# A two-layer hybrid transformer: tile rows of their own for keys, values and queries, with head sums and rotations inside later slabs

## The reference, cut to what matters

```python
hx = rmsnorm(x, g_pre1[i]) * (1.0 + sc1) + sh1
ux = hx @ w_in[i]
qx = apply_axial_rope(rmsnorm(split_heads(ux[..., :Q_END], N_Q_HEADS), q_norm[i]), rope)
kx, vx = kv_heads(ux[..., Q_END:V_END], k_norm[i], rope)
k_all = jnp.concatenate([kc, kx], axis=1)
v_all = jnp.concatenate([vc, vx], axis=1)
yx = mixer_out(qx, k_all, v_all, ux[..., V_END:P_END], ux[..., P_END:C_END], ux[..., C_END:], lp)
```

## Time and profile before

| | us |
|---|---|
| median of 3 runs | 2336.59 |
| lowest, highest | 2327.56, 2337.27 |
| the profiled execution, its own time | 2337.91 |
| its span, first to last instruction | 2336.1 |
| PE busy in the span | 2143.4 |
| DVE, POOL, ACT busy in the span | 1322.1, 740.4, 737.5 |

### The profile page before, as it was taken

One profiled execution on the slowest core, in us unless ns is written; L12 is line 12 of the kernel. 1 busy time (PEld: TensorE's weight loads), 2 busy tenths in 40 slices (PEclk: granted clock), 3 DMA queues, 4 the chain that ended last, 5 costly groups with the idle time before them and its releaser, 6 DMA issues.

```text
span 2336.1 us, 27666 instructions
## 1 busy us (share of the span) xinstructions
PE 2143.4 (92%) x11298; PEld 1824.1 (78%) x11298; DVE 1322.1 (57%) x1707; ACT 737.5 (32%) x1055; POOL 740.4 (32%) x336
## 2 busy tenths in 40 slices
PE   7889999899999699999999968898879997999997
PEld 6777788678888588888888856677658876888885
DVE  6459899843586566846516544798964314101114
ACT  2447511133222322221112224562124334222222
POOL 3220035132332332222222233103334444444442
PEclk9999999899999699999999978999889997999998
DMA  7110012021344233533223221101222232333322
GB/s 283 37 45 1 19 46 73 22 69 64 122 154 148 78 117 122 172 112 136 99 82 106 93 99 38 44 1 63 73 62 86 100 114 69 98 99 99 98 85 70
DMA packets 62910, 204.44 MB, mean 88 GB/s; under 512 B 7104, under 2 KB 8256, under 8 KB 62528
## 3 DMA queue, kind: packets, MB, share of 16 engines
q1 hardware_dynamic: 56592, 187.72, 24.1%
q10 hardware_dynamic: 6192, 14.95, 1.7%
HBM read 197.40 MB, written 5.24 MB: 87 GB/s over the span
## 4 chain that ended last, share of the span: by engine, by line
PE 70%; DVE 23%; ACT 3%; issue 2%; POOL 1%; DMA 0%; ACTq 0%; DVEq 0%
PE ps L444 61%; DVE conv_acc L1300 11%; PE ps L462 3%; DVE unit_stats L1261 2%; DVE pt0l L1281 1%; DVE pt1l L1281 1%; DVE probs L1275 1%; DVE norm_tmp L1121 1%; PE ps L493 1%; PE ps L615 1%; PE ps L513 1%; PE ps L474 1%; DVE x L1130 1%; PE ps L484 1%; PE ps L636 1%
## 5 line engine op out<-in xcount | busy, mean ns | idle before, releaser
L375 POOL TENSOR_TENSOR w_l<-w_raw,w_h 128x1024 fp32r<-128x1024 f32 (+2 forms) x296 | 675.0, 2283 | 1448.9 <-ACT w_h L749 1448.6
L444 PE MATMUL ps<-h_h,w_h 128*128 128x512 f32 (+1 forms) x1968 | 604.0, 362 | 21.9 <-ACT t L941 17.0
L444 PE MATMUL ps<-h_h,w_l 128*128 128x512 f32 (+1 forms) x1968 | 597.9, 358 | 0.0
L444 PE MATMUL ps<-h_l,w_h 128*128 128x512 f32 (+1 forms) x1968 | 594.3, 357 | 0.0
L444 PEld LDWEIGHTS ps<-h_h,w_h 128*128 128x128 f32 x1968 | 373.9, 190 | 86.1 <-ACT t L941 18.4
L444 PEld LDWEIGHTS ps<-h_l,w_h 128*128 128x128 f32 x1968 | 374.3, 190 | 56.7 <-issue 1.2
L444 PEld LDWEIGHTS ps<-h_h,w_l 128*128 128x128 f32 x1968 | 373.1, 190 | 55.0
L749 ACT ACTIVATE w_h<-w_raw 128x1024 fp32r<-128x1024 f32 (+2 forms) x296 | 281.1, 950 | 207.0 <-PE ps L444 182.6
L1300 DVE SCALAR_TENSOR_TENSOR conv_acc<-conv_in,vec,conv_acc 128x783 f32<-128x783 f32 (+1 forms) x240 | 269.3, 1169 | 2.8
L1163 DVE CUSTOM_DVE_ANT_0 ps<-ada_raw,c_row 128x1024 f32<-128x1024 f32 x160 | 265.1, 1657 | 9.6 <-DMA ada_raw<-in_ada 4.5
L444 PE MATMUL ps<-mid_h,w_l 128*128 128x512 f32 (+1 forms) x528 | 160.1, 358 | 0.0
(11 more groups left out here) (178 smaller groups left out, 2839.7 us busy)
## 6 DMA issues: line engine op xcount, KB each, us to landing
w_raw<-in_w SPq DMA_DIRECT2D x222, 512.0 KB, 3.5
ada_raw<-in_ada SPq DMA_DIRECT2D x80, 512.0 KB, 3.5
w_raw<-in_w SPq DMA_DIRECT2D x50, 256.0 KB, 2.6
ada_first<-in_ada SPq DMA_DIRECT2D x16, 512.0 KB, 6.7
x<-in_x ACTq DMA_DIRECT2D x16, 384.0 KB, 10.3
w_raw<-in_w SPq DMA_DIRECT2D x16, 384.0 KB, 3.0
x_between<-x ACTq DMA_DIRECT2D x8, 384.0 KB, 2.4
x<-x_between ACTq DMA_DIRECT2D x8, 256.0 KB, 5.4
```

Source lines behind the costliest of these rows:

```text
L375: nc.gpsimd.tensor_tensor(wl[:, s % RING, 0:n], raw[:, s % RAW, 0:n], wh[:, s % RING, 0:n], ALU.subtract).then_inc(split, 1)
L444: ins = nc.tensor.matmul(at(out, c0, c1), w[:, s % RING, b * P:(b + 1) * P], m[:, kt, c0:c1], start=(kt == 0 and n == 0), stop=(kt == n_k ...
```

## The change

- `t1`, `t2`, `t3` are no longer used for these tiles. A new layout of the region that also holds `acc` gives `qkv`, eight rows of 768: one for each of the six tiles (`value`), and two for squares and sine products (`squared`).
- Keys and values are two whole slabs of eight blocks, 0 and 1; queries are 2 to 5, and every later slab of a layer has a number lower by two. At the start slabs 2 and 3 are loaded whole.
- PSUM targets are k A[0], v A[1], q0 B, q1 A[0], q2 A[1], q3 B; the spread of k's root goes into OD.
- `gemm` takes hooks, work done behind a given block of the slab. Counting blocks from 0: k's head sums and rotation behind block 4 of q0, k's spread behind block 1 of q1, v's transposes behind block 6 of q1, q0's rotation behind block 1 of q2, q1's behind block 1 of q3, q2's behind block 2 of `cgate`, q3's behind block 2 of `cval`.
- ACT takes a tile out of PSUM (`evict`) ahead of the high parts of the tile before it (`high`), waiting only for the rotation two tiles back; `rounds` stands behind each eviction.

```diff
-S_KV, S_Q, S_CONV, S_P0, S_POOL, S_P1, S_P2, S_OUT, S_FF = 0, 4, 8, 16, 32, 40, 56, 72, 80
+S_KV, S_Q, S_CONV, S_P0, S_POOL, S_P1, S_P2, S_OUT, S_FF = 0, 2, 6, 14, 30, 38, 54, 70, 78
+            [("qkv", [KT, T], F32)])
+        IN_PSUM = {"k": A[0], "v": A[1], "q0": B, "q1": A[0], "q2": A[1], "q3": B}
+        def value(name):
+            return qkv[:, TILES.index(name)]
+        def squared(name):
+            return qkv[:, 6 + (0 if name == "k" else (int(name[1]) + 1) % 2)]
-                    load(2, 4)
-                    load(3, 4)
+                    load(2, KT)
+                    load(3, KT)
+                        if b == nb - 1:
+                            ins.then_inc(used, 1)
+                        if kt in hooks:
+                            hooks[kt]()
-                        gemm_pair(A, [(s, s + 1, 4), (s + 2, s + 3, 4)], pre_ready, full)
-                    elif name != "k":
-                        gemm(A[w], [(s0 + S_Q + n - 2, 8)], hh, hl, cols)
-                    if n:
-                        finish(tiles[n - 1])
+                gemm_pair(A, [(s0 + S_KV, s0 + S_KV + 1, KT)], pre_ready, full)
+                for n, (w, hooks) in enumerate((("B", {4: rotate("k")}), (0, {1: spread_k, 6: turn_v}),
+                                                (1, {1: rotate("q0")}), ("B", {1: rotate("q1")}))):
+                    take(w, "gemm", ly, f"q{n}")
+                    gemm(IN_PSUM[f"q{n}"], [(s0 + S_Q + n, 8)], hh, hl, cols, hooks=hooks)
-                gemm(A[0], [(s0 + S_CONV, 8)], hh, hl, cols)
-                finish(tiles[-1])
+                gemm(A[0], [(s0 + S_CONV, 8)], hh, hl, cols, hooks={2: rotate("q2")})
                 take(1, "cval", ly, 0)
-                gemm(A[1], [(s0 + S_CONV + 1, 8)], hh, hl, cols)
+                gemm(A[1], [(s0 + S_CONV + 1, 8)], hh, hl, cols, hooks={2: rotate("q3")})
```

161 lines of the change are left out of this document (88 added, 73 removed).

## The result

| | us |
|---|---|
| before, median of 12 runs | 2330.37 (2325.85 to 2337.56) |
| after, median of 12 runs | 2312.79 (2309.42 to 2321.47) |
| after divided by before, 95% interval | 0.9929 (0.991 to 0.9947) |
| profiled execution of after, its span | 2312.41, 2310.6 |

The change is faster by 0.7%, and by more than forecast: 2312.8 instead of 2323.5, just under the range's lower end of 2314. One fact about the runs is needed to read any of these numbers. The times of either kernel fall into two groups about 9 us apart: before 2325.9 to 2331.7 (7 of 12, median 2327.8) and 2336.0 to 2337.6 (5, median 2336.6); after 2309.4 to 2313.2 (7, median 2311.7) and 2320.3 to 2321.5 (5, median 2320.4). Group against group the change gives 16.1 and 16.2 us; the two medians of twelve lie 17.6 apart. The profiled execution of before (2337.91) was of the upper group, that of after of the lower.

A forecast was written before the change was run, and what follows sets the result against it. PE's sequence and the DVE and ACT chain it waits on bound the stage; 3.7 + 1.0 + 8.4 + 1.0 = 14.1, less 1.0 for clock, gives 13.1 us: 2337.9 to 2324.8, median 1.3 lower, 2323.5; range 2314 to 2331.

The forecast's parts named there:

- a rival with a chance of 0.09: Larger gain, 2316 us: waits ahead of other rotations and the slow clock in v's transposes count for more; chance 0.09.
- PE's way in layer 0: Layer 0's stage: PE reaches q3's head sums and rotation at 140.26 instead of 143.94, 3.68 us earlier.
- the chain from there to the scores: DVE and ACT from q3's rotation to the scores, 13.44 and 10.56 us before: one rounding less, 1.0 us in each layer.
- PE's way in layer 1: Layer 1's stage: PE reaches q3's head sums and rotation at 1464.37 instead of 1472.73, 8.36 us earlier.
- late at the hooks: Rival: k's root, spread and high parts come late, v's wait moves into q1, 6 us of gain go: 2329.5; chance 0.10.
- The step-through: Estimated layer 1 timeline in which no hook makes PE wait; a q tile takes 4.9 us against PE's 7.35.
- the prediction's signs: If right: k's last block to first scores about 71.2 us in layer 0, 50.8 in layer 1; PE idles 4 to 5 us.
- The rounding's 1.0 us in the chain: One rounding leaves the DVE and ACT chain ahead of the scores, standing behind an eviction instead: 1.0 us a layer.
- The lock: Rival: POOL splits block DVE's products, two collisions in a q tile, 5 us over three tiles of layer 1: 2328.5; chance 0.14.
- The clock: Longer PE gap ahead of the scores lowers the clock sooner: cost 0.5 us a layer, 1.0 in all, ends 0 and 3.
- the prediction's signs of being wrong: PE idle at a hook, DVE products over 2 us, clock near 0.5 over 10 us behind the scores, later first slab.
- The slower rival: The clock stays low in attention, where PE at 1.2 GHz becomes the bound: 2351 us; chance 0.05.

The follow-up runs named there:

- before_again: The unchanged kernel before, traced a second time; that execution took 2328.79 us.
- round_last: q3_in_gate with the weight roundings behind q1, q2 and q3 moved later, the last one behind the hyperbolic tangent; median 2309.65 us.
- q3_between: The changed kernel with q3's head sums and rotation moved from inside `cval` to behind the last block of `cgate`; median 2314.45 us.
- q3_in_gate: The changed kernel with q2's rotation behind block 1 and q3's behind block 6 of `cgate`, none in `cval`; median 2306.92 us, traced again 2310.87.
- the filled kernels: The changed kernel with 20 matmuls of unused result in PE's gap ahead of each layer's scores, traced twice; medians 2310.75 and 2310.66 us.

## Why the prediction was wrong

**The base: the step that took the forecast out of its range.** The forecast subtracted 13.1 us from the profiled 2337.9 and set it against a median of three runs, 2336.6. Both were of the upper group; the median of twelve is 2330.4. Of the 10.7 us between forecast and result, 6.2 are this; from 2330.4 the same 13.1 give 2317.3, inside the range. The other 4.5 are the gain, 17.6 between the medians for 13.1; 16.1 and 16.2 of it stand group against group, and the rest is where the medians of twelve fall in the two heaps. The three runs already lay 9 us apart, in two heaps, and "runs fall as low as the lowest of before did" stood only in a rival with a chance of 0.09.

**PE's way in layer 0, the term mis-sized: 3.68 forecast, 5.44 measured** from the pair's start to q3's group (82.00 before, 76.56 after), 4.74 from its end, while the chain from there to the scores came out at 12.48 us for a forecast of 12.44. The three periods with `cgate` and `cval` blocks took 33.92, as forecast to the hundredth. Three terms were off. v's transposes were entered with 1.16 us and a switch of 0.40. The row they came from stood at a granted clock of 0.50, behind the very wait that the change removes. At full clock q1's last block, the transposes and two blocks take 3.78 us, where the forecast had 4.68: 0.90. The spread and the blocks behind it took 6.79 for 7.13: 0.34. And the pair itself was 0.70 shorter, because the clock rose sooner in it (its slow pairs of 0.64 us are two fewer; its pace at full clock is 0.3533 in both traces); that is the execution's, not the change's. In before_again the clock did not fall behind the wait, and against that trace the way is only 2.5 us shorter. Elsewhere 0.2 us were lost.

**PE's way in layer 1: 8.36 forecast, 10.24 measured** (68.96 to 58.72), 9.84 from the pair's end, the chain 9.50 for 9.56. Again the transposes (2.73 for 3.64: 0.91), the spread (5.03 for 5.37: 0.34), the pair (0.40) and 0.11 in each of the three periods, less 0.10 elsewhere.

**Nothing late at the hooks.** The step-through held: no idle time at a hook in either layer. From k's last block to the scores it is 70.2 and 49.3 us, for 71.2 and 50.8 in the prediction's signs. The rounding's 1.0 us in the chain was right, as round_last shows from the other side (PE idle 0.95 and 0.94 us less).

**The lock.** It happened, once a tile: 2.67 and 2.08 us for two of layer 1's products in after, the longer one (DVE, then the split on POOL) here:

```profile
1435.06 2.67 DVE L1238 TENSOR_TENSOR qkv<-qkv,const 128x512 f32<-128x512 f32 x1
```

```profile
1434.78 2.40 POOL L385 TENSOR_TENSOR w_l<-w_raw,w_h 128x1024 fp32r<-128x1024 f32 x1 [4.94 <-ACT w_h L760]
```

The rival needed two collisions in a tile. One made PE wait nowhere, because the cover was large enough, so the rival's 5 us did not come. In q3_between, with 2.06 us for q2's product, it already lengthens the chain of layer 1 by 1.05 us, and in q3_in_gate, where the cover was gone, by 1.7. The Trainium skill, SBUF — State Buffer, section Who interferes with whom, calls this port pair an exclusive lock; by that rule a collision costs up to a whole split, and the traces agree: 2.07 us lost beside splits of 2.41.

**The clock: 0.5 a layer forecast, 3.2 in layer 0 and nothing in layer 1 between the first two traces.** The gap ahead of the scores was sized well (4.48 and 4.14 us for about 4.3 and 4). Its price was not: the term came from the first 2.4 us of scores, but in layer 0 the low stretch went on for some 17 us. How much of that is the gap's doing is not shown: before_again has the same stretch and 115.29 us behind a gap of 2.17, the filled kernels have 2.6 us less by traces and no clear gain by run times. One of the prediction's signs of being wrong, a clock near 0.5 for more than 10 us behind the scores, did come, and in one trace of before as well. The slower rival did not come: from 171 on the clock is 1.00.

**The sum.** 13.1 forecast; +1.7 and +1.9 for the two ways, -2.7 and +0.5 for the clock make 14.5, close to what the two profiles show at the same pace (14.7). The groups of runs say 16.1 and 16.2. This agreement rests on one trace of before: 1.1 us of the two ways are the pair's, and with before_again in its place the two profiles lie 16.4 apart, with 3.4 us less between the stages of layer 0, 3.1 more between its attentions and 2.7 more between those of layer 1. The 1.5 us lie within what two executions of before differ by, and stay unassigned.

**A loss inside the change.** The prediction's remark that "rotating q3 three blocks later in `cval` already gave back 3.12 + 2.04 us in the sums above" was right: moving it back returned 3.2 us of stage in layer 0, and in layer 1 2.04 of PE's way, of which the lock took 1.05 back. The parts of the change, by single traces and from the pair's end: own rows with ACT's order and whole slabs -7.1 and -11.3 us, hooks for k and v -1.8 and -0.6, q3 inside `cval` +3.2 and +1.0; whole slabs alone are nothing that shows.

## What to carry to other kernels

When a wait is removed, take the durations behind it from rows at the clock that will then be granted, not from rows that the wait itself had slowed. Look at single runs, not only at their median: where they stand in two heaps, find the stretch that differs before anything is subtracted from a profile of unknown heap. A scratch buffer of its own for each tile, with the order of ACT that it allows, gave all of this gain and more, since PE's new order as a whole lost a little; how early the last tile of a chain is started, and what else stands in the queues ahead of the result that everyone waits for, decided the rest.
